# Sample attention in a hybrid decoder step: each sample's softmax and values in a pipeline with the next samples' scores

## The chip, the cores and the metric

One Trainium2 chip, one core. The time is that of one whole execution of the program on the device, in microseconds (us). Five engines work at once, each on a queue of its own: TensorE (PE; its weight loads are shown apart as PEld), VectorE (DVE), ScalarE (ACT), GpSimd (POOL) and SyncE (SP), which here only starts DMAs. They wait for each other by semaphores that are written out by hand. Each engine takes its instructions in the order in which the code issues them.

## The reference, cut to what matters

The program runs one step of a two-layer decoder trunk in float32 for a prompt of 1024 tokens and for 8 samples of one new token each. Layer 0 is a gated linear recurrence beside a sparse attention; layer 1 is a chunked gMLP. A squared-ReLU MLP follows each. What the change touches is the attention of the 8 sample tokens, and of its three branches (compressed, selected, window) mostly the selected one:

```
rank = where(valid, imp + BIG * forced, -BIG)
_, idx = lax.top_k(rank, k_top)                 # 16 blocks of 64 cached tokens
sc = einsum('btgrd,bgtkd->bgrtk', q, K_selected) * ATT_SCALE
pr = masked_softmax(sc, kmask)
o_sel = einsum('bgrtk,bgtkd->btgrd', pr, V_selected)
o_b = gate0 * o_cmp + gate1 * o_sel + gate2 * o_win
```

Each sample has 2048 cached tokens with 2 key/value heads of 64 and 8 query heads. The kernel computes scores over all 2048 cached tokens and the new one, and adds a large negative number where a block isn't selected. 8 samples times 8 heads give R = 64 score rows.

## The kernel before

The sample attention lies between the prompt's attention and the output projection of layer 0. Its functions are `sp_sample`, `pool_sample`, `pe_sample`, `act_sample` and `dve_sample`. An engine waits for steps of another by name: `PE_S`, `ACT_S` and `DVE_S` number the steps of each engine in the order in which it completes them, and `wait_ge(sP, PE_S["x"])` holds until TensorE has done step x and all before it.

`pool_sample` gathers the selected branch's rows: eight indirect DMAs a sample (line 1047, 128 rows of 2 KB each), keys and values side by side, into `srows`, which has two buffers. From sample 2 on it waits for the last transposes of sample b-2 and for the copy of that sample's values.

`pe_sample` first works on the compressed and the window branch. For the window, each sample's keys are transposed (line 2018), copied by ScalarE to `ktb` (2117), and multiplied by the queries (2098); then comes a softmax, and the values (2041). Then the selected branch: for each sample, when all its rows have landed, four groups of four key transposes (line 2054), 512 tokens a group. ScalarE copies a group to `ktb` (2126), and one score matmul per group follows, written behind the next group's transposes (2103). The query operand `qm[:, b, :]` holds the queries of sample b in its own 8 columns and zeros elsewhere, so that the eight samples' scores add up in four PSUM banks, one row for each sample and head. VectorE meanwhile copies each sample's values to `vhold` (`hold`, line 1983), so that the row buffer can be filled again. When all 32 groups are done, the new key's scores are made (2060), VectorE adds the mask (2205) and takes the maximum of each row (2210), ScalarE takes the exponential (2128), VectorE scales (2214), TensorE transposes the probabilities (2065), and the values follow for all samples (2076), then the way out (2081, 2083, 2091), ScalarE's and VectorE's halves of the result (2133, 2227), and `pe_about`, the output projection (267).

The projection's weights come in units of 512 KB: SP loads a unit to one of two raw buffers (206), POOL splits it into a high and a low part in two passes (237, 240), and four split units can stand ready. SP and POOL turn to them when the last selected transposes are done and the values held; SP reloads the hidden state (`sp_reload`) behind the fourth unit, when the attention's result is there.

Of the kernel before, what the change touches and what calls it, by code (L numbers as in the profile page):

```python
# [21 lines left out]
P = 128  # L22
D = 1024
SEQ = 1024
NB = 8
# [16 lines left out]
def build(nc, x_prompt, x_sample, cache_cmp, cache_sel, state_win, state_hgrn, page_table,  # L42
# [5 lines left out]
    with ctx:  # L48
# [1849 lines left out]
        vhold = at("vhold", R_G, [P, NB, 16, P])  # L1898
        srows = at("srows", R_W, [P, 2, NT, 512])
# [25 lines left out]
        def steps(*names):  # L1925

            return {n: i + 1 for i, n in enumerate(names)}

        PE_S = steps("qs", "qm", "kn", "cmp", "imp", "ptc", *[f"wk{b}" for b in range(NB)], "win",
                     "ptw", "pnw", *[f"sk{b}_{g}" for b in range(NB) for g in range(4)], "sel", "pts0", "pts1", "pns", "vals", "out",  # L1930
                     "shift")
        ACT_S = steps("qs", "qm", "cmp", *[f"wk{b}" for b in range(NB)], "win",
                      *[f"sk{b}_{g}" for b in range(NB) for g in range(4)], "sel", "pts1", "hi")
        DVE_S = steps("m8", "gg", "qe", "kn", "cmpmax", "pcs", "pgsel", "cmpw", "ptc", "winmax", "winp", "pnw",
                      "ptw", "pnwT", "selmax", "selp", "pns", "pts0", "pnsT", "o8", "osb", "lo")
# [4 lines left out]
        s_sr = [sem("selected_rows0"), sem("selected_rows1")]  # L1940
        s_vh = sem("values_held")
# [16 lines left out]
        def pool_sample(pool):  # L1958
# [18 lines left out]
        def hold(dve, b):  # L1977

            dve.wait_ge(s_sr[b % 2], 128 * (b // 2 + 1))
            if b == 0:  # L1980
                dve.wait_ge(sP, PE_S["pnw"])
            src = srows[:, b % 2, :, :].rearrange("p i (e x) -> p (i e) x", e=2)[:, :, P:2 * P]
            dve.tensor_copy(vhold[:, b, :, :], src).then_inc(s_vh, 1)

        def pe_sample(pe):
# [37 lines left out]
            for b in range(NB):  # L2023
                last = pe.matmul(psum[0:R, 3, 0:1], qm[:, b, :], kn[:, 1, b:b + 1], start=(b == 0), stop=(b == NB - 1))
            last.then_inc(sP, 1)
            pe.wait_ge(sD, DVE_S["winp"])
            for i in range(4):
                last = pe.transpose(psum[:, 4, i * R:(i + 1) * R], srow[:, i * P:(i + 1) * P], ident[0:R, 0:R])
# [7 lines left out]
            for b in range(NB):  # L2036
                c = slice(b * HB, b * HB + HB)
                pe.matmul(psum[:, 7, c], vcs[0:NCMP_S, b, :], ptc[0:NCMP_S, c], start=False, stop=False,
                          skip_group_check=True)
                for i in range(4):  # L2040
                    last = pe.matmul(psum[:, 7, c], wrow[:, b, i, P:2 * P], pts[:, i, c], start=False, stop=False,
                                     skip_group_check=True)
            last.then_inc(sP, 1)

            for b in range(NB):
                pe.wait_ge(s_sr[b % 2], 128 * (b // 2 + 1))
                for g in range(4):
                    n = 4 * b + g
                    if n >= 2:
                        pb, pg_ = divmod(n - 2, 4)  # L2050
                        pe.wait_ge(sA, ACT_S[f"sk{pb}_{pg_}"])
                    for q in range(4):
                        src = srows[:, b % 2, 2 * g + q // 2, :].rearrange("p (e x) -> p e x", e=2)[:, q % 2, 0:P]
                        last = pe.transpose(psum[:, 4 + n % 2, q * P:(q + 1) * P], src, ident[:, :])
                    last.then_inc(sP, 1)
                    if n >= 1:
                        sel_scores(pe, n - 1)
            sel_scores(pe, 4 * NB - 1)
            for b in range(NB):
                last = pe.matmul(psum[0:R, 6, 0:1], qm[:, b, :], kn[:, 0, b:b + 1], start=(b == 0), stop=(b == NB - 1))  # L2060
            last.then_inc(sP, 1)
            pe.wait_ge(sD, DVE_S["selp"])
            for half in range(2):
                for i in range(8):
                    last = pe.transpose(psum[:, 4 + half, i * R:(i + 1) * R],
                                        srow[:, (8 * half + i) * P:(8 * half + i + 1) * P], ident[0:R, 0:R])
                last.then_inc(sP, 1)
            pe.wait_ge(sD, DVE_S["pns"])
            pe.transpose(psum[0:NB, 6, 0:R], pnew[:, :], ident[0:R, 0:R]).then_inc(sP, 1)
            pe.wait_ge(sD, DVE_S["pnsT"])  # L2070
            pe.wait_ge(sA, ACT_S["pts1"])
            pe.wait_ge(s_vh, NB)
            for b in range(NB):
                c = slice(b * HB, b * HB + HB)
                for i in range(16):
# [489 lines left out]
```

## Time and profile before

| | us |
|---|---|
| median of 3 runs | 3145.98 (3137.71 to 3147.54) |
| profiled execution, its own time | 3148.4 |
| its span, first to last instruction | 3146.6 |
| mean granted TensorE clock | 0.957 |
| TensorE busy | 2966.8 (94%) |
| VectorE / ScalarE / GpSimd busy | 1184.5 / 619.9 / 1133.4 |

The span is what lies between the first and the last instruction of the profiled execution; its own time is a little longer. Times within the trace count from the span's start. The granted clock is a share of TensorE's full speed: 1.00 is 2.4 GHz, 0.50 is 1.2 GHz. A busy TensorE is not one at its peak. In rows of a timeline, "x4" is the number of instructions merged, and the bracket gives the engine's idle time before them and what ended it; the number after x counts records, of which a float32 matmul can leave two.

### The profile page before, as it was taken

Reading aid. Unit: us, or ns where it says so; the run is one execution under the profiler, and the core shown is the slowest. Engines: PE = TensorE matmul, PEld = TensorE weight load, DVE = VectorE, ACT = ScalarE, POOL = GpSimd, SP = SyncE. Lnnn points to the kernel's source line nnn. Section 1 sums busy time; section 2 is a strip of 40 time slices with the busy share of each in tenths; the row PEclk is TensorE's granted clock in tenths of the full one; section 3 lists DMA queues with packets and bytes.
Section 4 is the critical chain, followed back from the end, with each engine's and each line's share of the span. In section 5 each row is a group of like instructions: output and inputs, shape, how many; then the busy total and the mean of one; then the engine's idle time right before and its main releaser. Section 6 shows DMA issues by size and latency. Waiting matters only on the chain.

```text
span 3146.6 us, 46295 instructions
## 1 busy us (share of the span) xinstructions
PE 2966.8 (94%) x20022; PEld 2821.9 (90%) x20022; DVE 1184.5 (38%) x1236; ACT 619.9 (20%) x1046; POOL 1133.4 (36%) x593
## 2 busy tenths in 40 slices
PE   6999889998998769999999999999899999999999
PEld 6999878887887429999999999999899999999998
DVE  4121372335443120244443444415623444444344
ACT  3100014545555120201111000221112000111103
POOL 5332232400000361534444444533454444444442
PEclk9999998969999689999999999999999999999999
DMA  4111331400000452111111111131031111111111
GB/s 163 47 49 55 129 95 54 145 20 1 1 1 13 136 146 88 41 47 47 47 44 50 43 44 46 40 121 48 21 101 42 48 47 41 45 47 47 47 47 54
DMA packets 197981, 184.74 MB, mean 59 GB/s; under 512 B 7413, under 2 KB 181746, under 8 KB 196506
## 3 DMA queue, kind: packets, MB, share of 16 engines
q1 hardware_dynamic: 187610, 149.25, 15.1%
q0 software_dynamic: 10240, 33.56, 3.5%
q8 instruction: 104, 1.70, 0.2%
q14 instruction: 27, 0.22, 0.0%
HBM read 161.88 MB, written 25.09 MB: 59 GB/s over the span
## 4 chain that ended last, share of the span: by engine, by line
PE 80%; issue 8%; DVE 5%; POOL 3%; ACT 2%; DMA 1%; SPq 0%; POOLq 0%; DVEq 0%; ACTq 0%
PE psum L267 48%; PE psum L437 6%; PE psum L293 5%; PE psum L1393 4%; PE psum L1748 3%; PE psum L1727 2%; PE psum L281 2%; POOL srows L1047 1%; POOL whl L237 1%; PE psum L1377 1%; PE psum L1693 1%; PE psum L2076 1%; PE psum L1694 1%; POOL whl L240 1%; DVE nmax L1833 1%
## 5 line engine op out<-in xcount | busy, mean ns | idle before, releaser
L267 PE MATMUL psum<-xhi,whl 128*128 128x344 f32 x4704 | 877.7, 321 | 6.5 <-ACT frel L481 2.9
L237 POOL TENSOR_TENSOR whl<-wraw,zeroc 128x1024 fp32r<-128x1024 f32 x186 | 372.1, 2000 | 1211.3 <-PE psum L267 841.2
L267 PEld LDWEIGHTS psum<-xhi,whl 128*128 128x128 f32 x4704 | 768.5, 189 | 7.3 <-issue 6.6
L240 POOL TENSOR_TENSOR whl<-wraw,whl 128x1024 fp32r<-128x1024 f32 x186 | 501.4, 2695 | 14.6
L267 PE MATMUL psum<-xlo,whl 128*128 128x344 f32 x2352 | 501.8, 322 | 0.0
L267 PE MATMUL psum<-ahi,whl 128*128 128x344 f32 x2304 | 427.4, 319 | 0.2
L267 PEld LDWEIGHTS psum<-xlo,whl 128*128 128x128 f32 x2352 | 400.6, 190 | 0.0
L267 PEld LDWEIGHTS psum<-ahi,whl 128*128 128x128 f32 x2304 | 373.1, 188 | 4.6 <-DVE ftmp L502 3.9
L492 DVE CAST ahi<-frel 128x1032 fp32r<-128x1032 f32 x64 | 172.8, 2700 | 509.0 <-ACT frel L483 509.0
L481 ACT ACTIVATE frel<-psum 128x1032 f32<-128x1032 f32 x64 | 66.1, 1033 | 1192.9 <-PE psum L267 1192.8
L502 DVE TENSOR_TENSOR ftmp<-psum,fscale 128x1032 f32<-128x1032 f32 x128 | 157.6, 1231 | 324.7 <-PE psum L267 264.1
L267 PE MATMUL psum<-alo,whl 128*128 128x344 f32 x1152 | 243.9, 320 | 0.0
L1047 POOL DMA_INDIRECT srows<-in_cache_sel_kv,idx x64 | 65.3, 1021 | 425.3 <-DVE ob L1878 359.7
L293 PE MATMUL psum<-whl,xhi 128*128 128x256 f32 (+1 forms) x1200 | 213.9, 281 | 4.1 <-DVE kvst L903 2.9
L505 DVE TENSOR_TENSOR hT<-hT,ftmp 128x1032 f32<-128x1032 f32 x128 | 191.3, 1494 | 4.4
L267 PEld LDWEIGHTS psum<-alo,whl 128*128 128x128 f32 x1152 | 192.4, 188 | 0.0
L293 PEld LDWEIGHTS psum<-whl,xhi 128*128 128x128 f32 (+1 forms) x1200 | 174.3, 176 | 8.8 <-DVE kvst L903 3.1
L293 PE MATMUL psum<-whl,xlo 128*128 128x256 f32 (+1 forms) x600 | 167.7, 280 | 0.0
L1748 PE MATMUL psum<-kvp,ptb 128*128 128x64 f32 x1056 | 145.3, 285 | 1.9 <-ACT ptb L1797 1.8
L1833 DVE TENSOR_REDUCE nmax<-psum 128x1 f32<-128x640 f32 (+7 forms) x128 | 90.0, 706 | 151.1 <-PE psum L1700 151.0
L437 PE MATMUL psum<-ahi,whl 128*128 128x344 f32 x768 | 144.3, 320 | 0.0
L1748 PEld LDWEIGHTS psum<-kvp,ptb 128*128 128x128 f32 x1056 | 140.2, 207 | 4.0 <-ACT ptb L1797 3.0
(393 smaller groups left out, 3423.8 us busy)
## 6 DMA issues: line engine op xcount, KB each, us to landing
wraw<-in_w_ffn SPq DMA_DIRECT2D x128, 512.0 KB, 3.8
wraw<-in_w_in_ab SPq DMA_DIRECT2D x26, 512.0 KB, 3.5
h_spill<-hT SPq DMA_DIRECT2D x2, 4128.0 KB, 12.6
hT<-h_spill SPq DMA_DIRECT2D x8, 1032.0 KB, 9.4
wraw<-in_w_in_c SPq DMA_DIRECT2D x16, 512.0 KB, 4.0
xtok<-in_x_prompt SPq DMA_DIRECT2D x2, 2048.0 KB, 12.4
wrow<-in_state_win_kv SPq DMA_DIRECT2D x4, 1024.0 KB, 16.1
wraw<-in_w_out_ab SPq DMA_DIRECT2D x8, 512.0 KB, 4.3
```

What stands on the lines that cost most here:

```text
L237: pool.tensor_tensor(whl[:, s, 0, :], raw, zeroc[:, 0:1].to_broadcast([P, UNIT]), ALU.add).then_inc(w_hi, 1)
L240: pool.tensor_tensor(whl[:, s, 1, :], raw, whl[:, s, 0, :].bitcast(F32), ALU.subtract).then_inc(w_ready, 1)
L267: last = pe.matmul(psum[:, 3 * bset + c, 0:TC], w, rhs[ah][:, k0 + k, c * TC:(c + 1) * TC], start=(k == 0 and n == 0), stop=(k == kn - 1 a ...
L293: last = pe.matmul(psum[0:m, bank, 0:256].rearrange("m (a b) -> m a b", a=2), (xhi, xlo)[ah][:, k, lo:lo + m], w, start=(k == 0 and n == 0 ...
L437: last = pe.matmul(psum[:, 3 * n + c, 0:TC], w, (ahi, alo)[ah][:, k, c * TC:(c + 1) * TC], start=(k == 0 and p == 0), stop=(k == 3 and p = ...
L492: dve.tensor_copy(ahi[:, j, :], frel[:, j % 2, :]).then_inc(f_hi, 1)
L502: dve.tensor_tensor(thirds(ftmp[:, n % 2, :]), pset(n % 2), thirds(fscale[:, :]), ALU.mult)\
L505: dve.tensor_tensor(hT[:, n, :], hT[:, n, :], ftmp[:, n % 2, :], ALU.add).then_inc(f_h, 1)
L1047: pool.indirect_dma_start(out=dst[:, i % dst.shape[1], :], out_offset=None, in_=view, in_offset=bass.IndirectOffsetOnAxis(ap=idx[:, b * 8 ...
L1393: last = pe.matmul(o, w1c[:, k, j, :], xv[:, :, j % 8, s:s + n], start=(j == 0), stop=(j == 15))
L1748: last = pe.matmul(psum[:, bank, 64 * h:64 * h + 64], ptb[:, k % 2, b * P:(b + 1) * P], kvp[:, lo + b, c0:c0 + 64], start=(b == 0), stop=( ...
L1833: dve.tensor_reduce(nmax[:, k % 4:k % 4 + 1], s_, AX.X, ALU.max, negate=True).then_inc(p_nm, 1)
```

## The change

`srows` becomes four buffers of one sample each. Two of them take the place of `vhold`, and the hold copies are gone. POOL gathers samples 0 to 3 without waiting for scores (sample 2 waits for a step long before), and sample b from 4 on after the values of sample b-4.

The mask is spread out to all 2048 columns once (`smask`), by two VectorE copies behind the choice of blocks. The new keys' scores of the selected branch are made beside those of the window branch.

Each score matmul now starts and stops its own bank, in turn 0 and 1; the rows of other samples hold zeros there. VectorE adds the mask to each group's scores into one of three `srow` buffers (`ma`), and takes the sample's maximum (`mx`) behind its fourth group. ScalarE takes the exponential of sample b behind the second key copy of sample b+1 (`exp`). TensorE transposes the sample's probabilities (`pt`) and ScalarE copies its 8 columns of them (`pts`) behind the fourth group of sample b+2; the values (`v`) follow behind the fourth group of sample b+3, straight from the row buffer. The last samples' steps stand behind the last scores.

The probabilities are not scaled before the values: the sums are inverted at the end, and the scale goes into the small matrix `dsc` by which the values' results are brought back. SP and POOL turn to the projection's weights after `v5`.

```diff
         wrow = at("wrow", R_G, [P, NB, 4, 256])
-        vhold = at("vhold", R_G, [P, NB, 16, P])
-        srows = at("srows", R_W, [P, 2, NT, 512])
+        srows = [at(f"srows{x}", off, [P, NT, 512]) for x, off in
+                 enumerate((R_W, R_W + 16384, R_G + 32768, R_G + 49152))]
+        srow = at("srow", R_G, [R, 3, NK + 8])
+        pts = at("pts", R_G + 24704, [P, 2, 16, HB])
+        o8 = at("o8", R_G + 25728, [HB, NB, P])
+        dsc = at("dsc", R_G + 29824, [HB, NB, HB])
...
-        srow = at("srow", R_H + 19328, [R, NK + 1])
-        pts = at("pts", R_H + 27552, [P, 16, R])
-        o8 = at("o8", R_H + 19328, [HB, NB, P])
+        smask = at("smask", R_H + 19328, [R, NK])
...
+        def pe_selected():
+            order = []
+            for n in range(4 * NB):
+                order.append(f"sk{groups[n]}")
+                if n:
+                    order.append(f"ss{groups[n - 1]}")
+                if n % 4 == 3:
+                    j = n // 4
+                    order += [f"pt{b}" for b in (j - 2,) if b >= 0] + [f"v{b}" for b in (j - 3,) if b >= 0]
+            return order + [f"ss{groups[-1]}", "pt6", "v5", "pt7", "v6", "v7"]
+
+        def act_selected():
+            order = []
+            for n in range(4 * NB):
+                order.append(f"sk{groups[n]}")
+                if n % 4 == 1 and n > 4:
+                    order.append(f"exp{n // 4 - 1}")
+                if n % 4 == 3 and n // 4 >= 2:
+                    order.append(f"pts{n // 4 - 2}")
...
-                if b >= 2:
-                    pool.wait_ge(sP, PE_S[f"sk{b - 2}_3"])
-                    pool.wait_ge(s_vh, b - 1)
                 if b == 0:
                     pool.wait_ge(p_cb, GROUPS)
-                gather(pool, cache_sel[0], srows[:, b % 2, :, :], b, range(NT), s_sr[b % 2])
...
+                if b == 2:
+                    pool.wait_ge(sP, PE_S["qs"])
+                if b >= 4:
+                    pool.wait_ge(sP, PE_S[f"v{b - 4}"])
+                gather(pool, cache_sel[0], srows[b % 4], b, range(NT), s_sr[b % 4])
...
             for b in range(NB):
-                last = pe.matmul(psum[0:R, 3, 0:1], qm[:, b, :], kn[:, 1, b:b + 1], start=(b == 0), stop=(b == NB - 1))
+                pe.matmul(psum[0:R, 3, 0:1], qm[:, b, :], kn[:, 1, b:b + 1], start=(b == 0), stop=(b == NB - 1))
+            for b in range(NB):
+                last = pe.matmul(psum[0:R, 3, 1:2], qm[:, b, :], kn[:, 0, b:b + 1], start=(b == 0), stop=(b == NB - 1),
+                                 skip_group_check=True)
             last.then_inc(sP, 1)
...
+            def keys_back(n):
+                b, g = divmod(n, 4)
+                if g == 0:
+                    pe.wait_ge(s_sr[b % 4], 128 * (b // 4 + 1))
+                if n >= 2:
+                    pe.wait_ge(sA, ACT_S[f"sk{groups[n - 2]}"])
+                for q in range(4):
+                    last = pe.transpose(psum[:, 4 + n % 2, q * P:(q + 1) * P],
+                                        srows[b % 4][:, 2 * g + q // 2, 256 * (q % 2):256 * (q % 2) + P], ident[:, :])
+                last.then_inc(sP, 1)
+
+            def selected_scores(n):
+                pe.wait_ge(sA, ACT_S[f"sk{groups[n]}"])
+                if n >= 2:
+                    pe.wait_ge(sD, DVE_S[f"ma{groups[n - 2]}"])
+                pe.matmul(psum[0:R, n % 2, :], qm[:, n // 4, :], ktb[:, n % 2, :], start=True, stop=True).then_inc(sP, 1)
+
+            def probs_back(b):
+                pe.wait_ge(sA, ACT_S[f"exp{b}"])
+                if b >= 1:
+                    pe.wait_ge(sA, ACT_S[f"pts{b - 1}"])
+                for i in range(16):
+                    last = pe.transpose(psum[:, 2 + i // 8, (i % 8) * R:(i % 8 + 1) * R],
+                                        srow[:, b % 3, i * P:(i + 1) * P], ident[0:R, 0:R])
+                last.then_inc(sP, 1)
+
+            def selected_values(b):
+                pe.wait_ge(sA, ACT_S[f"pts{b}"])
+                if b == 4:
+                    pe.wait_ge(sD, DVE_S["o8a"])
+                for i in range(16):
+                    last = pe.matmul(psum[0:HB, 6, (b % 4) * P:(b % 4 + 1) * P], pts[:, b % 2, i, :],
+                                     srows[b % 4][:, i // 2, 256 * (i % 2) + P:256 * (i % 2) + 2 * P],
+                                     start=(i == 0), stop=(i == 15))
+                last.then_inc(sP, 1)
+
+            for n in range(4 * NB):
+                keys_back(n)
+                if n >= 1:
+                    selected_scores(n - 1)
+                if n % 4 == 3:
+                    j = n // 4
+                    if j >= 2:
+                        probs_back(j - 2)
+                    if j >= 3:
+                        selected_values(j - 3)
+            selected_scores(4 * NB - 1)
+            probs_back(6)
+            selected_values(5)
+            probs_back(7)
+            selected_values(6)
+            selected_values(7)
+            pe.wait_ge(sD, DVE_S["rscale"])
+            pe.matmul(psum[0:HB, 2, 0:NB], rmod[:, :], rscale[:, :], start=True, stop=True).then_inc(sP, 1)
+            pe.wait_ge(sD, DVE_S["pns"])
+            pe.transpose(psum[0:NB, 3, 0:R], pnew[:, :], ident[0:R, 0:R]).then_inc(sP, 1)
+            pe.wait_ge(sD, DVE_S["o8b"])
...
+            def exponential(b):
+                act.wait_ge(sD, DVE_S[f"mx{b}"])
+                act.activation(srow[:, b % 3, 0:NK + 1], srow[:, b % 3, 0:NK + 1], ACT.Exp, bias=smax[:, b:b + 1],
+                               accum_out=ssum[:, b:b + 1]).then_inc(sA, 1)
+
+            def probs(b):
+                act.wait_ge(sP, PE_S[f"pt{b}"])
+                if b >= 2:
+                    act.wait_ge(sP, PE_S[f"v{b - 2}"])
+                act.activation(pts[:, b % 2, :, :],
+                               psum[:, 2:4, :].rearrange("p a (i r) -> p (a i) r", r=R)[:, :, b * HB:(b + 1) * HB],
+                               ACT.Copy).then_inc(sA, 1)
+
+            act.wait_ge(sP, PE_S["win"])
             for n in range(4 * NB):
+                act.wait_ge(sP, PE_S[f"sk{groups[n]}"])
+                if n >= 2:
+                    act.wait_ge(sP, PE_S[f"ss{groups[n - 2]}"])
                 act.activation(ktb[:, n % 2, :], psum[:, 4 + n % 2, :], ACT.Copy).then_inc(sA, 1)
+                if n % 4 == 1 and n > 4:
+                    exponential(n // 4 - 1)
+                if n % 4 == 3 and n // 4 >= 2:
+                    probs(n // 4 - 2)
+            exponential(7)
+            probs(6)
+            probs(7)
...
+            did("pgsel")
+            for e in range(2):
+                o_ = smask[:, :].rearrange("r (a e p) -> r a e p", e=2, p=P)[:, :, e, :].rearrange("r a (q l) -> r a q l", l=32)
+                m_ = selneg[:, 0:32].rearrange("r (a q) -> r a q", q=4).unsqueeze(3).to_broadcast([R, 8, 4, 32])
+                if e == 0:
+                    link("dve", dve.tensor_copy(o_, m_))
+                else:
+                    step(dve.tensor_copy(o_, m_))
...
-            for b in range(NB):
-                hold(dve, b)
...
-            step(dve.tensor_scalar(srow[:, :], srow[:, :], sst[:, 8:9], None, ALU.mult))
+            def new_probs(b):
+                dve.wait_ge(sA, ACT_S[f"exp{b}"])
+                step(dve.tensor_copy(snew[:, b:b + 1], srow[:, b % 3, NK:NK + 1]))
+
+            for n in range(4 * NB):
+                b, g = divmod(n, 4)
+                dve.wait_ge(sP, PE_S[f"ss{groups[n]}"])
+                if g == 0 and b >= 3:
+                    did(f"ac{b - 3}")
+                    dve.wait_ge(sP, PE_S[f"pt{b - 3}"])
+                step(dve.tensor_tensor(srow[:, b % 3, 512 * g:512 * g + 512], psum[0:R, n % 2, :],
+                                       smask[:, 512 * g:512 * g + 512], ALU.add))
+                if g == 3:
+                    chained(dve.tensor_copy(srow[:, b % 3, NK:NK + 1], sfin[:, 0:1]))
+                    did(f"ma{groups[n]}")
+                    step(dve.tensor_reduce(smax[:, b:b + 1], srow[:, b % 3, 0:NK + 1], AX.X, ALU.max, negate=True))
+                if g == 1 and b >= 1:
+                    new_probs(b - 1)
+                if n == 4 * NB - 3:
+                    dve.wait_ge(sP, PE_S["v3"])
+                    step(dve.tensor_copy(o8[:, 0:4, :].rearrange("r b d -> r (b d)"), psum[0:HB, 6, :]))
+            new_probs(7)
+            did("ac7")
+            chained(dve.tensor_tensor(ssum[:, :], ssum[:, :], m8, ALU.mult))
+            chained(dve.tensor_reduce(sfin[:, 1:2], ssum[:, :], AX.X, ALU.add))
+            chained(dve.reciprocal(sfin[:, 2:3], sfin[:, 1:2]))
+            chained(dve.tensor_tensor(sfin[:, 3:4], sfin[:, 2:3], g64[:, 1:2], ALU.mult))
+            step(dve.tensor_scalar(rscale[:, :], m8, sfin[:, 3:4], None, ALU.mult))
+            did("rscale")
...
+            step(dve.tensor_copy(o8[:, 4:8, :].rearrange("r b d -> r (b d)"), psum[0:HB, 6, :]))
...
-            sp.wait_ge(sP, PE_S["sk%d_3" % (NB - 1)])
-            sp.wait_ge(s_vh, NB)
+            sp.wait_ge(sP, PE_S["v5"])
...
-            pool.wait_ge(sP, PE_S["sk%d_3" % (NB - 1)])
-            pool.wait_ge(sA, ACT_S["sk%d_3" % (NB - 1)])
-            pool.wait_ge(sP, PE_S["sel"])
+            pool.wait_ge(sP, PE_S["v5"])
```

## Rows read from the trace of the kernel before

**Rows 1.** The page: span and instructions, then shares of the chain by engine

```profile
span 3146.6 us, 46295 instructions
PE 80%; issue 8%; DVE 5%; POOL 3%; ACT 2%; DMA 1%; SPq 0%; POOLq 0%; DVEq 0%; ACTq 0%
```

**Rows 2.** Windows: from:to, length, busy us per engine, granted clock, DMA share, GB/s

```profile
1038.20:1076.40 38.20, 34.14 (x150) 25.10 (x151) 3.12 (x10) 5.59 (x10) 0.00 (x0) 0.68 0.17 56
1076.40:1158.60 82.20, 62.79 (x198) 24.31 (x199) 9.72 (x8) 19.10 (x32) 49.49 (x48) 0.83 0.53 155
1158.60:1173.70 15.10, 2.92 (x32) 2.63 (x31) 11.60 (x10) 2.69 (x3) 12.09 (x6) 0.65 0.45 129
1173.70:1203.30 29.60, 29.59 (x256) 23.57 (x256) 0.00 (x0) 0.00 (x0) 5.62 (x3) 0.95 0.00 1
```

**Rows 3.** Timeline: start, length, engine, line; first matmul behind the changed stage

```profile
1208.15 1.23 PE L267 MATMUL psum<-xhi,whl 128*128 128x344 f32 x3 [0.56 <-DVE xlo L2227]
```

**Rows 4.** Timeline of POOL: first, one slow and last of 48 gather issues

```profile
1083.33 0.94 POOL L1047 DMA_INDIRECT srows<-in_cache_sel_kv,idx  x1 [46.69 <-PE psum L2054]
...
1095.83 1.85 POOL L1047 DMA_INDIRECT srows<-in_cache_sel_kv,idx  x1 [0.30 <-issue]
...
1146.19 0.95 POOL L1047 DMA_INDIRECT srows<-in_cache_sel_kv,idx  x1 [0.30 <-issue]
```

**Rows 5.** Timeline of TensorE: score groups at full clock, and behind two waits

```profile
1082.40 0.66 PE L2054 MATMUL psum<-ident,srows 128*128 128x128 f32 x4
1082.99 1.07 PE L2103 MATMUL psum<-ktb,qm 128*64 128x512 f32 x2
1083.99 0.66 PE L2054 MATMUL psum<-ident,srows 128*128 128x128 f32 x4
...
1095.67 1.12 PE L2054 MATMUL psum<-ident,srows 128*128 128x128 f32 x4 [5.25 <-DMA srows<-in_cache_sel_kv,idx]
1096.71 1.97 PE L2103 MATMUL psum<-ktb,qm 128*64 128x512 f32 x2
...
1128.41 0.66 PE L2054 MATMUL psum<-ident,srows 128*128 128x128 f32 x4 [2.34 <-DMA srows<-in_cache_sel_kv,idx]
1129.00 1.96 PE L2103 MATMUL psum<-ktb,qm 128*64 128x512 f32 x2
```

**Rows 6.** Timeline: a key copy, and the softmax over all samples

```profile
1156.74 0.60 ACT L2126 ACTIVATE ktb<-psum 128x512 f32<-128x512 f32 x1 [0.99 <-PE psum L2054]
...
1159.48 2.47 DVE L2205 TENSOR_TENSOR srow<-psum,selneg 64x1024 f32<-64x1024 f32 x2 [8.37 <-PE psum L2060]
...
1162.17 2.28 DVE L2210 TENSOR_REDUCE sst<-srow 64x1 f32<-64x2049 f32 x1
1164.48 2.00 ACT L2128 ACTIVATE srow<-srow,sst 64x2049 f32<-64x2049 f32 x1 [7.14 <-DVE sst L2210]
...
1171.02 1.97 PE L2065 MATMUL psum<-ident,srow 64*128 64x64 f32 x16 [11.57 <-DVE srow L2214]
```

**Rows 7.** Windows inside the values, columns as in Rows 2

```profile
1177.70:1179.70 2.00, 2.00 (x21) 1.64 (x20) 0.00 (x0) 0.00 (x0) 1.70 (x1) 1.00 0.03 8
...
1183.70:1203.00 19.30, 19.30 (x179) 15.91 (x178) 0.00 (x0) 0.00 (x0) 0.00 (x0) 1.00 0.00 1
```

**Rows 8.** Timeline: a wide product, the new-key matmuls, two hold copies

```profile
1025.85 1.22 DVE L2154 TENSOR_TENSOR qe<-qrow,m 64x1024 f32<-64x1024 f32 x1 [7.38 <-DMA g<-gate_scratch]
...
1053.06 1.04 PE L2024 MATMUL psum<-kn,qm 128*64 128x1 f32 x16
...
1076.91 2.36 DVE L1983 COPY vhold<-srows 128x2048 f32<-128x2048 f32 x2 [18.01 <-PE psum L2041]
```

**Rows 9.** Timeline: the next units' weight loads, the first split's two passes

```profile
1156.74 13.54 SPq L206 DMA_DIRECT2D wraw<-in_w_out_ab  x4
...
1161.31 1.89 POOL L237 TENSOR_TENSOR whl<-wraw,zeroc 128x1024 fp32r<-128x1024 f32 x1 [14.17 <-DMA wraw<-in_w_out_ab]
1163.27 2.34 POOL L240 TENSOR_TENSOR whl<-wraw,whl 128x1024 fp32r<-128x1024 f32 x1
```

More of the change, by code:

```diff
@@ L1934, in build @@
-        DVE_S = steps("m8", "gg", "qe", "kn", "cmpmax", "pcs", "pgsel", "cmpw", "ptc", "winmax", "winp", "pnw",
-                      "ptw", "pnwT", "selmax", "selp", "pns", "pts0", "pnsT", "o8", "osb", "lo")
+        groups = [f"{b}_{g}" for b in range(NB) for g in range(4)]
+        def pe_selected():
[8 more added lines that the diff above has]
+            return order + [f"ss{groups[-1]}", "pt6", "v5", "pt7", "v6", "v7"]
@@ new lines, in build @@
+        PE_S = steps("qs", "qm", "kn", "cmp", "imp", "ptc", *[f"wk{b}" for b in range(NB)], "win",
+                     "ptw", "pnw", *pe_selected(), "sc", "pns", "out", "shift")
+        ACT_S = steps("qs", "qm", "cmp", *[f"wk{b}" for b in range(NB)], "win", *act_selected(), "hi")
+        DVE_S = steps("m8", "rmod", "gg", "qe", "kn", "cmpmax", "pcs", "pgsel", "smask", "cmpw", "ptc", "winmax", "winp", "pnw",
+                      "ptw", "pnwT", *dve_selected(), "rscale", "pns", "pnsT", "dsc", "o8b", "osb", "lo")
@@ L1939, in build @@
         s_wr = [sem(f"window_rows{b}") for b in range(4)]
-        s_sr = [sem("selected_rows0"), sem("selected_rows1")]
-        s_vh = sem("values_held")
+        s_sr = [sem(f"selected_rows{x}") for x in range(4)]
         s_m16 = sem("row_mask")
@@ L2027, in pe_sample @@
             for i in range(4):
[L2028 removed]
+                last = pe.transpose(psum[:, 4, i * R:(i + 1) * R], wprob[:, i * P:(i + 1) * P], ident[0:R, 0:R])
             last.then_inc(sP, 1)
@@ L2040, in pe_sample @@
                 for i in range(4):
-                    last = pe.matmul(psum[:, 7, c], wrow[:, b, i, P:2 * P], pts[:, i, c], start=False, stop=False,
+                    last = pe.matmul(psum[:, 7, c], wrow[:, b, i, P:2 * P], ptw[:, i, c], start=False, stop=False,
                                      skip_group_check=True)
             last.then_inc(sP, 1)
-            for b in range(NB):
[L2046 to L2057, printed above, removed]
@@ L2058, in pe_sample @@
-            sel_scores(pe, 4 * NB - 1)
-            for b in range(NB):
[L2060 to L2075, printed above, removed]
-                    last = pe.matmul(psum[0:HB, b // 4, (b % 4) * P:(b % 4 + 1) * P], pts[:, i, c], vhold[:, b, i, :],
-                                     start=(i == 0), stop=(i == 15))
@@ L2078, in pe_sample @@
-            last.then_inc(sP, 1)
-            pe.wait_ge(sD, DVE_S["o8"])
-            for b in range(NB):
-                pe.matmul(psum[:, 7, b * HB:(b + 1) * HB], o8[:, b, :], ident[0:HB, 0:HB], start=False, stop=False,
+            def keys_back(n):
[8 more added lines that the diff above has]
+                last.then_inc(sP, 1)
```

87 lines of the change are left out of this document (35 added, 52 removed).

## The prediction

> **What bounds the kernel now.** I read the page's span and chain first [rows 1]: 80% of the chain is TensorE, so whatever holds TensorE back in one stage and is not given back later reaches the end. Then one window for each step of the sample attention [rows 2]. The window branch takes 38.2 us, the eight samples' selected scores 82.2, the softmax over all samples 15.1, the values 29.6, the way out 4.8; the next layer's matmuls start at 1208.15 [rows 3]. So the changed stage, from the first selected transposes at 1076.4 to there, is 131.7 us.
>
> In the 82.2 us of scores TensorE is busy for 62.8 only. The gathers' rows say why [rows 4]: POOL issues one every 1.25 us (0.95 busy, 0.30 between), 48 of them from 1083.33 to 1147.1 without a break, and TensorE starts samples 2 to 7 when their eighth tile lands. That stage is bound by POOL's issuing, not by the number of buffers: with two, a buffer is free before POOL comes to it. The softmax window has TensorE busy for 2.9 of its 15.1 us, and the values run behind it with nothing beside them. Those two, 44.7 us together, are what a pipeline could cover.
>
> **The order of the new queues, which decides.** POOL fills four buffers at once, then waits for the values of sample b-4 before it gathers sample b. In TensorE's written order those values, v0, come after all scores of sample 3, and the very next instruction is the first transpose of sample 4, whose rows POOL may begin to fetch only now. The same holds for v1 and sample 5, v2 and 6, v3 and 7: values, then the whole gather with TensorE idle, then scores. ScalarE and VectorE have no work either, because the last score group of the sample before is queued behind that transpose. Before, six gathers were partly covered; now samples 0 to 3 cost no gather wait and samples 4 to 7 each cost a whole one.
>
> **Terms.** Durations are the rows' own.
>
> 1. One whole gather: POOL was released when sample 0's last transposes ended (1082.40 + 0.66 [rows 5]), issued at 1083.33, and TensorE started on the landed rows at 1095.67 [rows 4, 5]: 12.6 us. Four times: 50.4. Nothing else is on POOL then and no hold copy runs; I take this as it stands (by the mean pitch of 1.34 us over the 48 it would be 13.2).
>
> 2. Score groups. Transposes and scores of one group follow at 0.59 and 1.00 us at the full clock (1082.40, 1082.99, and the next group at 1083.99 [rows 5]): 1.59 a group, 6.36 a sample. At half clock the transposes take 1.04 (1095.67 to 1096.71) and the scores 1.97 less the 0.07 by which the next group overlaps them, 2.95 a group [rows 5].
>
> 3. Softmax chain of one sample. From the end of its last scores: mask add of 512 columns, 0.65 (half of the mean 1.23 of the 1024 wide one); the new key's column 0.22; the maximum over 2049 columns 2.28; exponential 2.10 with its start; then, because ScalarE's queue holds it in front of the next key copy, that copy, 0.60; with five hand-overs of about 0.06, 6.2 us [rows 6]. In TensorE's order three transpose groups and two score groups stand between, 3.7 us. So scores wait 2.5 us in each of samples 1 to 3. VectorE's own queue (maximum, then the next mask add) is late by less than that.
>
> 4. Probabilities back, 16 transposes of 64 rows: 1.97 us at half clock after an 11.6 us wait [rows 6]; at full clock I take 1.1. Values of one sample, 32 records: at full clock 179 records took 19.3 us [rows 7], so 3.45. The moved operand has the same 128 contiguous columns as the held copy, so no change there.
>
> 5. Samples 0 to 3: 7.6 for sample 0 as before (1076.4 to 1083.99 [rows 2, 5]); 6.36 + 2.5 = 8.9 for sample 1; 10.0 with the first probabilities; 13.4 with the next ones and v0: 39.9. The clock: a wait of 2.34 us was followed by scores at half (1.96 us for one group at 1129.00, against 1.07 [rows 5]). So the 2.5 us waits should each cost one slow group, 1.36; three make 4. Sum 43.9, bounds 39 and 49.
>
> 6. Samples 4 to 7, each: the gather, 12.6; the first two groups at half clock (as after 5.25 us in [rows 5]). The held-back scores of the sample before end at 3.0; the chain of 6.2 from there lets the third group start at 9.2, so the slow clock hides behind the chain; scores 1.1, probabilities 1.1, values 3.45: 15.0, and 0.5 for a clock that may fall once more. 28.1 each, 112.4 for four.
>
> 7. After v4: last scores 1.07, chain and the probabilities' copy before it 5.9, the eighth probabilities 1.1, v6 and v7 6.9 (v5 stands in the chain's shadow): 15.0.
>
> 8. Way out: 4.8 before. The copy of the values is half as wide, 512 columns for 1024 (0.6 less, by the 1.23 us of [rows 6] for that width), and one small matmul, one transpose and two small VectorE steps come in, at about 0.25 to 0.3 each: 5.3. VectorE's scale chain lies beside v6.
>
> 9. Before the stage. Two mask copies of 64x1024 now stand on the path to the window branch: 0.6 each at the rate of the held copy (2.36 for two of 2048 columns), 1.2 at that of the 1024 wide product [rows 8], and up to 0.95 each where POOL is inside a gather; I take 2.3, bounds 1.2 and 4.4. The eight new-key matmuls move here from behind the scores: 1.04 [rows 8], plus 0.2 to copy the column. The gathers of samples 2 and 3 now run beside the window softmax, some 0.5. Sum 4.0, bounds 2.5 and 7.
>
> On the last item there is a row and a rule. A gather issued as a hold copy ran took 1.85 us against 0.95 [rows 4]. The Trainium skill ("SBUF — State Buffer", SBUF: two separate sides) says that such a VectorE copy keeps GpSimd off the port pair it needs to write descriptors. By that rule removing the eight holds gives POOL five times 0.9 back, 4.5 us, were POOL still the bound; here it isn't, since TensorE's order is, and the term stays nought.
>
> **What goes, and what it is worth.** The eight holds go off VectorE (1.2 us each, beside TensorE's work). The final scale over 2049 columns, part of the 11.6 us for which [rows 6]'s transposes waited, goes. Values of v0 to v5 no longer stand behind one softmax, but they stand in front of gathers. Weight units: SP and POOL now wait for v5 where they waited for the last transposes. A unit landed and began to split 4.6 us after its issue (1156.74 to 1161.31 [rows 9]) and its split is 1.9 + 2.3 us, so the first is ready 8.9 us after v5; TensorE wants it 14.7 us after v5 (1.4 of wait, 1.1, 6.9, 5.3). The rest come faster than the matmuls use them. Cost nil, margin 5.8; without it, up to 3.
>
> **The sum.** 43.9 + 112.4 + 15.0 + 5.3 = 176.6 against 131.7: 44.9 more, and 4.0 before the stage: 48.9. The profiled execution took 3148.4 us (span 3146.6), so 3197.3; the median of the runs is 2.4 lower: 3195. Item bounds: -5 and +5 on item 5, about -4 and +8 on item 6, -1.5 and +3 on item 9, and 2 or 3 of drift between runs. Likeliest case: 3182 to 3212.
>
> **Rivals.**
>
> A, four buffers hide the gathers (not slower). Place: the four waits ahead of samples 4, 5, 6 and 7. It decides if POOL's wait for v0 is passed about 12 us before TensorE reaches sample 4. Then four gathers (50.4) go, but with no idle time the chain stalls each sample (13.4 as sample 3, plus 1.4), so the stage is 43.9 + 59.2 + 15.0 + 5.3 = 123.4: 8.3 less, plus 4.0: 3142 on the median's footing. For it: POOL had samples 0 and 1 ready long ahead, and four rather than two are now. Against it: the waits name v0 to v3, and each is one TensorE instruction ahead of the transposes that need the rows. The Trainium skill ("Perfetto Trace Analysis", Optimization Strategy) holds that a gap that repeats can mean too few buffers. By that rule the six gaps before would be the target and this case the right one. The rows don't bear it out: POOL had no gap, so a buffer was never what it waited for. 6%.
>
> B, the clock stays at half through samples 4 to 7. TensorE is idle for nearly half of the time there. Then probabilities cost 2.0 rather than 1.1, values 6.9 rather than 3.45, scores 2 rather than 1.1: 5.3 more a sample, 21 for four: 3216. For it: the whole window stage runs at a mean of 0.68 [rows 2]. Against it: behind the 15.1 us window with its waits the values were at 1.00 from 1177.7 on, 4 us after their start [rows 7]. 13%.
>
> C, the gather overlaps in part with work that I count behind it, since the chain and the slow clock cover each other: the stage before sample 4 without slow groups, the mask copies at the fast rate, and the scores at full clock after the wait. 4 + 2 + 4 x 1.5 off: 3183. 17%.
>
> **Chances.** Forecast 64, C 17, B 13, A 6. What this kernel's measurement tells from no change is about 0.3%, 9 us. Forecast, B and C are slower by far more. A at 3142 lies within; with luck in its chain it would be faster, so I split it: faster 3, same 3, slower 94. The range that holds 8 in 10 goes from 3180 to 3214: it takes in the forecast and most of C, and leaves out A and most of B.
>
> **What would show it.** In the new trace: gathers of samples 2 and 3 directly behind those of 0 and 1, ending near 1057; TensorE without gather waits until v0 near 1124; four waits of about 12 us ahead of the transposes of samples 4 to 7, released by the gather; eight-gather bursts on POOL with some 15 us between; scores of each sample's third group waiting for ScalarE's key copy, which follows the exponential; next layer's first matmul near 1257. Wrong if the gather waits are under 5 us, if the gap between v0 and sample 4 holds other TensorE work, or if a later stage starts less than 30 us late.

## The result, and the profile after

The changed kernel took 3189.39 us in the median (3182.7 to 3195.03, 4 runs) against 3146.76 for the kernel before: ratio 1.0148, 95% interval 1.0119 to 1.0177 (the two medians alone are 42.6 us apart, a ratio of 1.0135). It is slower, by 1.5%. The forecast was 3195 us, 48.9 more. In a second set of runs the ratio was 1.0155 (1.0126 to 1.0185).

The span of the profiled execution went from 3146.6 to 3193.2. Where the 46.6 us came from, read off both timelines (the last column is from one more trace of each kernel, in that second set):

| us | before | after | second pair, before / after |
|---|---|---|---|
| up to the first selected gather | 1016.2 | 1011.1 | 1014.4 / 1005.3 |
| from there to the first selected transposes | 60.4 | 66.5 | 60.5 / 62.9 |
| from there to the next layer's first matmul | 131.5 | 173.7 | 131.6 / 169.1 |
| the rest | 1938.4 | 1941.8 | 1939.3 / 1941.6 |

The third row is called the stage below, and the second the front. The stage is where the change costs: 42.2 and 37.5 us. The first and last rows differ between runs of every kernel here (1005 to 1024, and 1938.4 to 1942.0, in no order of the kernels) and lie outside the change. The stage's start before and after, and its end after ([rows 3] has its end before):

```profile
1076.66 1.95 PE L2054 MATMUL psum<-ident,srows 128*128 128x128 f32 x8
...
1077.68 1.95 PE L2090 MATMUL psum<-ident,srows 128*128 128x128 f32 x8
...
1251.39 1.23 PE L267 MATMUL psum<-xhi,whl 128*128 128x344 f32 x3 [0.56 <-DVE xlo L2318]
```

The windows that answer to [rows 2] are those of samples 0 to 3 with v0, then of samples 4 to 7 with v1 to v4, then of the end (columns as there):

```profile
1077.70:1120.60 42.90, 37.30 (x159) 17.54 (x159) 17.27 (x24) 15.70 (x24) 0.00 (x0) 0.82 0.00 0
1120.60:1231.50 110.90, 55.48 (x289) 29.12 (x289) 21.03 (x29) 18.12 (x28) 30.32 (x32) 0.74 0.28 76
1231.50:1251.40 19.90, 17.18 (x169) 13.59 (x168) 5.53 (x15) 2.73 (x5) 9.99 (x5) 0.97 0.29 83
```

In the middle one TensorE is busy for half of the time. POOL's timeline, where [rows 4] had an unbroken row of gathers, has bursts of eight; here are the last of the first four samples' and both ends of the next one, then the first of sample 5:

```profile
1050.76 0.94 POOL L1047 DMA_INDIRECT srows<-in_cache_sel_kv,idx  x1 [0.30 <-issue]
1120.76 0.94 POOL L1047 DMA_INDIRECT srows<-in_cache_sel_kv,idx  x1 [69.05 <-PE psum L2114]
...
1129.52 0.95 POOL L1047 DMA_INDIRECT srows<-in_cache_sel_kv,idx  x1 [0.30 <-issue]
1148.04 0.95 POOL L1047 DMA_INDIRECT srows<-in_cache_sel_kv,idx  x1 [17.57 <-PE psum L2114]
```

POOL waits for line 2114, the values. TensorE's side of sample 4 (line 2090 is the key transposes, 2098 the scores, 2105 the probabilities back, 2114 the values):

```profile
1116.82 3.66 PE L2114 MATMUL psum<-srows,pts 128*8 128x128 f32 x32
1133.19 1.12 PE L2090 MATMUL psum<-ident,srows 128*128 128x128 f32 x4 [12.70 <-DMA srows<-in_cache_sel_kv,idx]
1134.23 1.97 PE L2098 MATMUL psum<-ktb,qm 128*64 128x512 f32 x2
...
1139.85 0.66 PE L2090 MATMUL psum<-ident,srows 128*128 128x128 f32 x4
1141.97 1.07 PE L2098 MATMUL psum<-ktb,qm 128*64 128x512 f32 x2 [1.47 <-ACT ktb L2194]
1142.97 1.21 PE L2105 MATMUL psum<-ident,srow 64*128 64x64 f32 x16
1144.11 3.66 PE L2114 MATMUL psum<-srows,pts 128*8 128x128 f32 x32
1160.53 1.12 PE L2090 MATMUL psum<-ident,srows 128*128 128x128 f32 x4 [12.77 <-DMA srows<-in_cache_sel_kv,idx]
```

TensorE makes the values, stands idle for 12.7 us, transposes at half clock, waits shortly for ScalarE's key copy, does the probabilities and the values, and so on for each sample. The four gather waits are 12.70, 12.77, 12.70 and 12.60: 50.8 us. VectorE and ScalarE between (the answer to [rows 6]) show why the third group waits: in ScalarE's queue the exponential stands ahead of the key copies, and itself waits for VectorE's maximum.

```profile
1136.24 0.68 DVE L2289 TENSOR_TENSOR srow<-psum,smask 64x512 f32<-64x512 f32 x1 [19.76 <-PE psum L2098]
1137.03 2.28 DVE L2294 TENSOR_REDUCE smax<-srow 64x1 f32<-64x2049 f32 x1
1139.34 2.01 ACT L2178 ACTIVATE srow<-srow,smax 64x2049 f32<-64x2049 f32 x1 [1.46 <-DVE smax L2294]
1141.34 1.06 ACT L2194 ACTIVATE ktb<-psum 128x512 f32<-128x512 f32 x2
```

### The profile page after: what moved, and what is told of

Read it like the earlier page. It is cut to its first block, busy times and chain, and to the rows that moved or that the text cites. A ratio compares the mean times of both kernels' runs of the same rounds, so it can differ in the third digit from the quotient of the medians.

```text
span 3193.2 us, 46673 instructions
## 1 busy us (share of the span) xinstructions
PE 2977.8 (93%) x20136; PEld 2827.1 (89%) x20136; DVE 1207.5 (38%) x1287; ACT 634.8 (20%) x1067; POOL 1132.0 (35%) x593
## 4 chain that ended last, share of the span: by engine, by line
PE 80%; issue 8%; DVE 5%; POOL 3%; DMA 2%; ACT 2%; SPq 0%; POOLq 0%; DVEq 0%; ACTq 0%
PE psum L267 47%; PE psum L437 6%; PE psum L293 5%; PE psum L1393 4%; PE psum L1748 3%; PE psum L1727 2%; PE psum L281 2%; PE psum L2098 1%; POOL whl L237 1%; PE psum L2114 1%; PE psum L1377 1%; PE psum L1693 1%; POOL srows L1047 1%; PE psum L1694 1%; DMA wrow<-in_state_win_kv 1%
## 5 line engine op out<-in xcount | busy, mean ns | idle before, releaser
L1047 POOL DMA_INDIRECT srows<-in_cache_sel_kv,idx x64 | 61.4, 960 | 497.6 <-DVE ob L1878 355.8
## 6 DMA issues: line engine op xcount, KB each, us to landing
h_spill<-hT SPq DMA_DIRECT2D x2, 4128.0 KB, 12.6
```

Of the source, the lines that this page charges most:

```text
L1047: pool.indirect_dma_start(out=dst[:, i % dst.shape[1], :], out_offset=None, in_=view, in_offset=bass.IndirectOffsetOnAxis(ap=idx[:, b * 8 ...
```

## The experiments

The theory was that of the forecast: each of the last four gathers stands whole in TensorE's way, since the values that release it stand just before the transposes that need it. Beside it, the softmax chain (mask add, maximum, exponential, the key copy behind it) holds each sample's third group. The rivals: the time is the softmax chain's or the slow clock's, or POOL's.

Experiments 1 to 4 ran together on one chip, on which the kernel before took 3161.7 us, 15 more than at first. The expectations in absolute times don't fit that chip, so ratios and stages are what to read. The changed kernel itself was not run there; experiment 4 leaves its stage as it is, and that took 173.9 us, against 173.7 and 169.1 in the two traces of the changed kernel. So a stage is good to some 5 us.

**1. The late gathers left out.**

```
-                if b >= 4:
-                    pool.wait_ge(sP, PE_S[f"v{b - 4}"])
-                gather(pool, cache_sel[0], srows[b % 4], b, range(NT), s_sr[b % 4])
+                if b < 4:
+                    gather(pool, cache_sel[0], srows[b % 4], b, range(NT), s_sr[b % 4])
...
-                    pe.wait_ge(s_sr[b % 4], 128 * (b // 4 + 1))
+                    pe.wait_ge(s_sr[b % 4], 128)
```

> The changed kernel with the gathers of samples 4 to 7 left out (their scores and values are made from the rows of samples 0 to 3, so the selected branch of those samples is wrong); every other instruction and its order stay. Theory (each of the four gathers stands whole in TensorE's way): the four waits of 12.6 to 12.8 us go and nothing takes their place; the stage from the first selected transposes to the next layer goes from 173.9 to 121-124 us, the time to 3137 (3130 to 3144). Rival (the softmax chain through VectorE and ScalarE, or a slow clock, takes most of the waits' place): only 15 to 25 us go, 3164 to 3175.

The time was 3171.2 us, ratio to the kernel before 1.0028 (1.0015 to 1.004). As a time that is the rival's and not the theory's, but by the ratios (1.0028 for 1.0148) some 38 us of the whole time went. The stage took 128.2: 45.7 us less than 173.9, far more than the rival gave and 4 to 7 less than the theory had. The timeline tells where those are. Sample 4's end, for the one shown above:

```profile
1154.98 1.32 PE L2097 MATMUL psum<-ktb,qm 128*64 128x512 f32 x2 [2.00 <-ACT ktb L2193]
1156.22 1.97 PE L2104 MATMUL psum<-ident,srow 64*128 64x64 f32 x16
1158.12 5.78 PE L2113 MATMUL psum<-srows,pts 128*8 128x128 f32 x32
```

Behind the 2.00 us wait the clock is now half, and it falls on the probabilities (1.97 for 1.21) and the values (5.78 for 3.66). In the changed kernel the clock was slow too, but right behind the gather wait, where the chain was awaited anyhow. Over v0 to v4 the values alone took 9.6 us more than 5 x 3.66 here (5.03, 5.78, 6.13, 5.08, 5.83).

**2. Probabilities and values one sample sooner.** All gathers stay; only the place of two steps in TensorE's queue moves, with the copy of the probabilities in ScalarE's and, in VectorE's, the copy that frees the values' bank. TensorE's part:

```
-                    if j >= 2:
-                        probs_back(j - 2)
-                    if j >= 3:
-                        selected_values(j - 3)
+                    if j >= 1:
+                        probs_back(j - 1)
+                    if j >= 2:
+                        selected_values(j - 2)
```

> The changed kernel with the probabilities' transposes and the values of each sample one sample sooner in the order of every queue (values of sample b behind the scores of sample b+2); all gathers stay. Theory: POOL is released for sample 4 before sample 3's scores (about 13 us of TensorE work), so a gather of 12.6 us is nearly hidden and the four waits shrink to 0-2 us each: 3142 (3134 to 3150). Rival (POOL or the DMA path is the bound, four gathers cost their time wherever they stand): over 3175. Second rival (the probabilities aren't ready so soon, a wait on ScalarE's exponential of 2-4 us a sample comes in): 3155 to 3170.

The time was 3181.2 us, ratio 1.0057 (1.0038 to 1.0075). As a time that is the first rival's (over 3175), and by the ratios some 29 us of the whole went, less than the theory's 47. But the stage took 130.7 us: 43.2 less, with the same 64 gathers. The whole times of both experiments hold a front of 81 to 83 us as well, 15 longer than at first (experiment 4). TensorE's waits in this stage, by whom it waited for (us in total, times, longest), hold no gather any more; the longest:

```profile
PE psum L2098 <- ACT ktb L2192: 12.0, 6, 2.0
PE psum L2098 <- issue: 2.4, 1, 2.4
PE psum L2105 <- ACT srow L2176: 1.7, 1, 1.7
```

So it was the order, not the gathers' own time. What is left are the chain's 2 us in six samples and the slow clock behind them: values of 5.09, 5.83, 4.82, 5.21, 5.95 and 4.92 us for 3.66.

**3. The exponential one group later.** VectorE's copy of the new key's probability, which waits for it, moves along. ScalarE's part:

```
-                if n % 4 == 1 and n > 4:
+                if n % 4 == 2 and n > 4:
                     exponential(n // 4 - 1)
```

> The changed kernel with each sample's exponential one group later in ScalarE's queue (behind the third key copy of the next sample in place of the second), so that it no longer waits for the maximum in front of a key copy. Theory: TensorE's waits of 2.0, 2.0, 1.5, 1.5, 1.9, 0.8 and 0.7 us on the key copy go, 10 us, and 1-2 us of slow clock with them; the gather waits stay at 12.7: 8 to 12 us less than the changed kernel, 3179. Rival (the exponential holds the next copy for its own 2.1 us wherever it stands): within 3 us of 3189.

The stage took 156.9 us, 17.0 less than 173.9 (12.2 less than 169.1), where 8 to 12 were expected. The whole time, 3203.4 and a ratio of 1.0129 (1.0109 to 1.0149), can't be told from the changed kernel's 1.0148; it has the longer front in it (next experiment). The waits on the key copy added up to 10.2 us in the changed kernel. All but one of 0.3 us are gone, and the exponential does fit between two key copies. The rest of the gain is clock: steps that were slow behind those waits now run at full rate. Sample 2's third scores and the probabilities behind them, which took 1.43 and 1.97 before:

```profile
1123.25 1.04 PE L2098 MATMUL psum<-ktb,qm 128*64 128x512 f32 x2
1124.22 1.22 PE L2105 MATMUL psum<-ident,srow 64*128 64x64 f32 x16
```

The gather waits stayed (12.79, 12.55, 12.80, 12.71).

**4. The gathers of samples 2 and 3 behind the window scores.**

```
                 if b == 2:
-                    pool.wait_ge(sP, PE_S["qs"])
+                    pool.wait_ge(sP, PE_S["win"])
```

> The changed kernel with the gathers of samples 2 and 3 held back until the window scores are done. Theory (they share the DMA engines with the window rows' load and delay it): the wait of 2.8 us for the window rows goes, with the slow groups behind it; from the first gather to the first selected transposes 62 to 64 us in place of 66.3, and samples 2 and 3 still don't wait. Rival (the window rows arrive late for another cause): 66 us stays.

This was a single run of 3205.4 us, so its trace is what counts. On this chip the front was 81.5, 83.4 and 83.2 us in the three kernels above, whose instructions up to there are the changed kernel's, and 68.1 here; in the first trace it was 66.5. So some 14 us went where 3 were expected, and the stage behind was the 173.9 us used above. In experiment 2's trace the front looks like this (who waited, for whom, us in total, times, longest; "remote" and "issue" are waits that no engine's work ended):

```profile
ACT ktb L2170 <- remote: 23.9, 2, 15.4
...
DVE sst L2227 <- remote: 9.0, 1, 9.0
...
PE psum L2042 <- issue: 6.7, 1, 6.7
...
PE psum L2156 <- issue: 6.2, 1, 6.2
PE psum L2156 <- ACT ktb L2170: 6.1, 1, 6.1
```

Over the 9 us wait the DMA engines ran at a share of 1.06 and 369 GB/s; over the two behind it (1052 to 1058 and 1061 to 1067) only 285 and 103 GB/s were moved. With the two gathers moved, the waits on the window's key copies and scores (2170, 2156) are gone; the 9 us one ahead of them, where gathers 0 and 1 meet the window rows, stays (10.4). The rate alone is not the cause: in the changed kernel's first trace there were 370 GB/s too, from 1030 to 1040, and none of these waits. What was awaited stays open. It came in one set of runs of the three in which this order of gathers was traced.

**5. Both kernels again, and what beats them.** The first two are the kernels unchanged:

> The kernel before, unchanged, for its trace on the chip and in the job of the next runs (in the first such job the kernel before took 15 us more than where it was first profiled). Theory: the stage from the first selected transposes to the next layer takes 131.7 us as before; if the whole time is longer again, the extra lies ahead of it, between the first gather and the first selected transposes (60.2 us in the first trace), as waits for code or for the window rows. Rival: everything is longer in proportion.

> The changed kernel, unchanged. Ratio to the kernel before 1.012 to 1.018; the stage from the first selected transposes to the next layer 172 to 176 us; ahead of it 66 us, or some 80 if the waits seen in the last job come with the gathers of samples 2 and 3.

On this chip the kernel before took 3147, its stage 131.6 and its front 60.5, so the 15 us that it had taken more on the chip of experiments 1 to 4 could not be traced. (In all four traces from there the first selected gather starts at 1021.0 to 1021.8, against 1005.3 to 1016.2 in the four traces of the table, so part of the 15 may lie ahead of anything told here.) The changed kernel came to 1.0155 (1.0126 to 1.0185), with a stage of 169.1 us, a little under the range given, and a front of 62.9.

The third kernel joins experiments 2 and 3, with the values another two groups sooner, so that a gather has six groups for cover, and the last scores ahead of the seventh probabilities:

```
...
+                if n % 4 == 1 and n // 4 >= 2:
+                    selected_values(n // 4 - 2)
+                if n == 4 * NB - 1:
+                    selected_scores(n)
+                if n % 4 == 3 and n // 4 >= 1:
+                    probs_back(n // 4 - 1)
...
```

> The changed kernel with the exponential one group later, the probabilities' transposes behind the next sample's scores, each sample's values behind the second group of the sample after that, and the last scores ahead of the seventh probabilities. Theory (gather waits and chain waits were the whole loss, and the slow clock came from them): TensorE has 8 x (6.4 + 1.2 + 3.6) = 90 us of work at full clock, the first groups 3 more, the end 5.3 and its waits 2: 100 to 106 us for the stage in place of 173.9; with 5 to 6 us more ahead of it the time is 0.992 to 0.996 of the kernel before. Rival (the clock falls anyway, as VectorE's maximum or ScalarE's exponential hold each sample once): 115 to 125 us, 0.998 to 1.002.

Ratio 0.9928 (0.9905 to 0.9951). The stage takes 104.0 us in place of 169.1, and TensorE is busy for nearly all of it at a clock of 0.94:

```profile
1074.90:1178.80 103.90, 96.81 (x614) 56.30 (x614) 50.41 (x68) 36.79 (x57) 47.08 (x40) 0.94 0.35 102
```

The fourth adds experiment 4's edit and puts the two mask copies behind the compressed branch's last copy.

> y1 with the gathers of samples 2 and 3 behind the window scores and the two mask copies behind the compressed probabilities' copy. Theory: 2 to 5 us less than y1 where the window rows' load is in the way, up to 14 where instruction loads are too (x4 had its first selected transposes 14 us sooner than x2): 0.988 to 0.994. Rival: POOL ends the gather of sample 3 only some 22 us after the window scores, so that sample 2 or 3 waits and the gain is lost.

Ratio 0.9892 (0.9857 to 0.9928), 3114.1 us: the best here, 1.1% under the kernel before and 2.6% under the changed one by the two ratios. Its front took 61.4 us against 65.1, its stage 103.4. The two intervals overlap, and the profiled spans were equal (3117.9 and 3117.8, with the rest 3.1 us longer), so the last edits' share is seen in the front only. A sample in its steady state, with no wait in it and POOL's gather running beside:

```profile
1116.63 0.66 PE L2093 MATMUL psum<-ident,srows 128*128 128x128 f32 x4
...
1119.96 1.21 PE L2108 MATMUL psum<-ident,srow 64*128 64x64 f32 x16
...
1124.28 3.66 PE L2117 MATMUL psum<-srows,pts 128*8 128x128 f32 x32
1127.87 0.66 PE L2093 MATMUL psum<-ident,srows 128*128 128x128 f32 x4
```

11.24 us a sample; the same steps with the gather wait took 27.3.

**6. The hold copies on ScalarE, in the kernel before.** The forecast said that POOL's issuing bounds its scores, and that a hold copy on VectorE keeps POOL. Each hold copy now follows the first key copy of its sample in ScalarE's queue.

```
...
-            dve.tensor_copy(vhold[:, b, :, :], src).then_inc(s_vh, 1)
+            act.activation(vhold[:, b, :, :], src, ACT.Copy).then_inc(s_vh, 1)
```

> The kernel before with the eight hold copies moved from VectorE to ScalarE, behind the first key copy of their sample; nothing of the change in it. Theory (POOL's issuing bounds the scores, and a hold copy on VectorE keeps one gather of each sample at 1.85 us for 0.95): all 48 gathers run 1.25 us apart, the last is issued 4 to 5 us sooner, the stage of 131.7 us becomes 127 to 128, and the time 0.998 to 0.999 of the kernel before. The Trainium skill's page SBUF — State Buffer states the rule of the port pair that this rests on. Rival 1 (the slow gather has another cause, such as the semaphore traffic at a landing): the 1.85 stays and nothing is gained. Rival 2 (ScalarE's copy of about 1.9 us delays each sample's second key copy and TensorE with it): POOL gains, TensorE gives it back, 0.999 to 1.001.

The stage took 128.0 us against 131.5 and 131.6: 3.5 less, at the edge of what was expected (127 to 128). The slow gathers are gone (minimum, median and maximum of 64, in ns; the kernel before had 1882 for a maximum):

```profile
L1047 POOL DMA_INDIRECT srows<-in_cache_sel_kv,idx x64: 942/946/1034, 1024.1 to 1151.3; - x64
L1983 ACT ACTIVATE vhold<-srows x8: 1901/1902/1902, 1085.9 to 1156.0; 128x2048 f32<-128x2048 f32 x8
```

So the first rival (another cause) is out. The whole time, 0.9994 (0.9971 to 1.0018), can't tell 3.5 us from none. POOL now waited twice for TensorE (1.3 and 1.0 us), so it is barely the bound.

## Why the prediction was right, and by how much its terms were off

The step that carried it held: with the release of gather b in front of sample b's transposes in one queue, four buffers hide nothing from sample 4 on. Experiments 1 and 2 show it from two sides, 45.7 and 43.2 us of the stage. The signs that it named came: eight gathers in a burst with 17.6 to 19.6 us between (15 were forecast), four waits of 12.6 to 12.8, and the next layer 43.2 us later. Rival A failed where the prediction said, at the place of v0 in the order. Experiment 2 is that rival with the order put right; its stage of 130.7 us is 7 longer than A's 123.4, as the chain's waits still drop the clock. The third and fourth kernels of experiment 5 move the chain too, and with 104.0 and 103.4 us they are worth more than A promised.

By terms, forecast and measured (first pair):

| term | forecast | measured |
|---|---|---|
| four gathers (1) | 50.4 | 50.8 |
| samples 0 to 3 with v0 (5) | 43.9 | 42.8 |
| samples 4 to 7 with v4 (6) | 112.4 | 111.1 |
| after v4 (7) | 15.0 | 14.8 |
| way out (8) | 5.3 | 5.0 |
| the stage | 176.6 | 173.7, second pair 169.1 |
| ahead of it (9) | +4.0 | +6.1, second pair +2.4 |

The chain's waits came to 2.0, 2.0 and 1.5 us in samples 1 to 3 where item 3 had 2.5, as the new key's column, the exponential's start and the hand-overs took less than I had them at; the mask add did not (0.68 for 0.65). Item 5's slow groups were there, behind the waits of samples 1 and 2. In the second pair samples 4 to 7 took 109.3 us rather than 111.1 and samples 0 to 3 took 40.0 rather than 42.8: the chain's waits were 7.8 us in all, not 10.2, and the first of 2.00 us had no slow group behind it. So how much clock these waits cost differs from run to run, within item 5's bounds of 39 and 49. Item 9 had about the right size by luck. The mask copies took 0.69 us each, 1.2 together, not 2.3; in their place came a wait for the window rows that the prediction did not have. It let the two moved gathers meet the window softmax, and not the window rows' load:

```profile
1047.44 0.66 PE L2053 MATMUL psum<-ident,wrow 128*128 128x128 f32 x4 [2.75 <-DMA wrow<-in_state_win_kv]
```

Slow groups follow it. In the second pair this wait is 2.25 us, with none behind it. The two gathers are its cause: in experiment 5's third kernel it is 2.54 us, and in the fourth, with them moved, there is none, nor in the kernel before. (The mask copies that the fourth moves as well only let TensorE ask for the rows sooner.)

Rival B (half clock through samples 4 to 7) did not come: values took 3.66 us in all but one (5.06). Rival C (3183) came in part: the mask copies ran at its fast rate, but the scores behind each gather wait at half clock (1.97), and the median, 3189.4, lies midway between C and the forecast. The rule that the prediction took from the Trainium skill ("SBUF — State Buffer", SBUF: two separate sides) agrees with experiment 6 (longest gather 1.03 us for 1.88) and changed nothing here, as said. Its price of 4.5 us for the kernel before was a little high: the five slow gathers took 1.85, 1.81, 1.88, 1.88 and 1.40 us, 4.1 in all over 0.95.

What the prediction took from the Trainium skill on repeating gaps ("Perfetto Trace Analysis", Optimization Strategy) was dismissed too fast. The prediction holds that POOL never waited for a buffer, but the first row of [rows 4] has 46.69 us of just that: the gather of sample 2 waited for sample 0's last transposes. From there on POOL's pitch made the gaps, 19.4 us in six waits. With four buffers and the values early enough, in the last two kernels of experiment 5, no gather wait is left. So the buffers were worth having, and it was their place in the order that made them a loss; what the better order would do with two buffers was not run.

The prediction wrote that the slow clock hides behind the chain in item 6, and it did. Experiment 1 shows the other side: take the gather wait away and the slow clock comes out from behind it, 9.6 us on the values.

## What to carry to other kernels

More buffers help only as far as their release stands ahead of their next use in the order of the engine that does both: write down, for each buffer, the instruction that frees it and the one that needs it refilled, and count the work between; here it was none, against a refill of 12.7 us. In a hand-ordered pipeline, a long instruction goes behind the short ones that other engines wait for: one place further for an exponential took 12 to 17 us off the stage. And a wait of 2 us costs more than itself when TensorE's clock is half behind it; how much depends on which matmuls come next.

## What the runs showed of the hardware that was not expected

- Waits of 1.5 to 2 us on ScalarE were often followed by matmuls at half clock, 1.2 GHz for 2.4 (experiment 3: 10.2 us of waits, 12 to 17 of time), but not always: in the changed kernel the one of 1.48 us and the 1.47 us one above were followed by scores at full rate (1.07). In its second trace so was one of 2.00, where the same scores took 1.64 in the first:

```profile
1082.59 1.07 PE L2098 MATMUL psum<-ktb,qm 128*64 128x512 f32 x2 [2.00 <-ACT ktb L2194]
```

- While gathers and the window rows' load were under way, engines stood for 6 to 9 us at a time on one chip with nothing in the trace to wait for, and the front took 81.5 to 83.4 us, against the 66.5 and 62.9 us that the same instructions took in two other sets of runs. The DMA engines moved 369 GB/s over the first such wait and 103 over the last, so their rate does not explain it. The cause is open.
- With a VectorE copy of 128x2048 beside it, a gather's issue took 0.9 us more (1.85 for 0.95); the same copy on ScalarE takes 1.90 us for 1.23, and no gather beside it took over 1.03.
